# Two hybrid layers on one core: where key, query and output transposes and the conformer sums stand in PE's order

## What is computed

```python
for l in range(DEPTH):                         # DEPTH = 2
    u_lat = h_lat * (1.0 + scale) + shift      # the context likewise
    q, k, v, z_a, s_b, s_c, s_h, z_s, c_a, c_g, z_c, g_m = split(u_lat @ w_in[l])
    q, k = rope(rms_norm(q)), rope(rms_norm(k))          # 8 query heads, 2 key heads of 64
    o_attn = softmax(q @ k_all.T / 8) @ v_all            # keys: 256 context + 1024 latent
    br_a = (o_attn * silu(z_a)) @ w_pa
    br_b = (s_b * dwconv3(s_c * s_h) * silu(z_s)) @ w_ps
    hc = dwconv31(c_a * sigmoid(c_g)) + b_cdw
    hc = silu(layer_norm(hc, cln_g, cln_b))
    br_c = (hc * silu(z_c)) @ w_pc + b_pc
    merged = sigmoid(g_a) * br_a + sigmoid(g_b) * br_b + sigmoid(g_c) * br_c
    h_lat = layer_norm(alpha * h_lat + gate * (merged @ w_o), ...)
```

## Time and profile before

| | |
|---|---|
| median of 3 runs | 2879.9 us (2878.3 to 2881.78) |
| the profiled execution | 2872.59 us |
| its span, first to last instruction | 2870.8 us |
| mean granted PE clock | 0.978 |
| busy: PE, DVE, POOL, ACT | 93%, 53%, 32%, 29% |

### The profile page before, as it was taken

One profiled execution on the slowest core, in us unless ns is written; L12 is line 12 of the kernel. 1 busy time (PEld: TensorE's weight loads), 2 busy tenths in 40 slices (PEclk: granted clock), 3 DMA queues, 4 the chain that ended last, 5 costly groups with the idle time before them and its releaser, 6 DMA issues.

```text
span 2870.8 us, 32327 instructions
## 1 busy us (share of the span) xinstructions
PE 2677.8 (93%) x13560; PEld 2197.1 (77%) x13560; DVE 1511.9 (53%) x1410; ACT 820.9 (29%) x1156; POOL 907.0 (32%) x819
## 2 busy tenths in 40 slices
PE   7999999999999999999995899999999999999993
PEld 4778888887887888788883677777788888877882
DVE  3454444441019988845626444554540199875635
ACT  3234444442100000142213434444441000014313
POOL 3431111111225333334531342111113355544550
PEclk8999999999999999999998999999999999999996
DMA  6010110011241111133343311101012211123421
GB/s 253 30 61 34 34 37 34 34 43 57 75 163 65 32 43 38 48 118 121 128 162 133 135 48 46 40 34 41 34 41 81 74 52 44 45 70 125 144 95 66
DMA packets 65521, 212.12 MB, mean 74 GB/s; under 512 B 7520, under 2 KB 10848, under 8 KB 63328
## 3 DMA queue, kind: packets, MB, share of 16 engines
q1 hardware_dynamic: 47520, 179.11, 17.8%
q10 hardware_dynamic: 17856, 30.94, 2.9%
HBM read 164.93 MB, written 45.09 MB: 73 GB/s over the span
## 4 chain that ended last, share of the span: by engine, by line
PE 83%; DVE 7%; ACT 6%; issue 2%; DMA 1%; POOL 1%; SPq 0%; ACTq 0%; DVEq 0%; POOLq 0%
PE PS L695 46%; PE PS L824 19%; PE PS L855 5%; PE PS L864 5%; PE PS L877 5%; DVE cv L1487 2%; ACT Pr L1118 2%; ACT PTh L1138 1%; PE PS L887 1%; DVE qTl L1420 1%; DVE e L1555 1%; PE PS L736 1%; PE PS L742 1%; DMA wmA<-wmod 1%; DVE e L1563 1%
## 5 line engine op out<-in xcount | busy, mean ns | idle before, releaser
L584 POOL CAST wh<-wraw 128x512 fp32r<-128x512 f32 (+1 forms) x376 | 297.7, 792 | 1476.5 <-PE PS L695 805.6
L586 POOL TENSOR_TENSOR wl<-wraw,wh 128x512 fp32r<-128x512 f32 (+1 forms) x376 | 534.3, 1421 | 30.1
L1454 DVE TENSOR_TENSOR PTl<-PS,PTh 128x512 fp32r<-128x512 f32 x328 | 226.9, 692 | 423.1 <-ACT PTh L1138 423.1
L1487 DVE SCALAR_TENSOR_TENSOR cv<-hc,vec,cv 128x1024 f32<-128x1024 f32 x360 | 441.7, 1254 | 8.2
L695 PE MATMUL PS<-Uh,wh 128*128 128x512 f32 (+1 forms) x1536 | 428.3, 377 | 17.0 <-ACT Uh L1023 15.7
L695 PE MATMUL PS<-Uh,wl 128*128 128x512 f32 (+1 forms) x1536 | 420.1, 371 | 0.0
L695 PE MATMUL PS<-Ul,wh 128*128 128x512 f32 (+1 forms) x1536 | 418.9, 371 | 0.0
L824 PE MATMUL PS<-Uh,wh 128*128 128x512 f32 (+1 forms) x960 | 358.4, 373 | 1.2 <-ACT stg L1076 1.2
L824 PE MATMUL PS<-Ul,wh 128*128 128x512 f32 (+1 forms) x960 | 359.3, 374 | 0.0
L824 PE MATMUL PS<-Uh,wl 128*128 128x512 f32 (+1 forms) x960 | 359.0, 374 | 0.0
L1138 ACT ACTIVATE PTh<-PS 128x512 fp32r<-128x512 f32 x328 | 196.4, 599 | 480.0 <-PE PS L864 479.0
(11 more groups left out here) (153 smaller groups left out, 3275.8 us busy)
## 6 DMA issues: line engine op xcount, KB each, us to landing
wraw<-w SPq DMA_DIRECT2D x140, 512.0 KB, 3.4
graw<-stg ACTq DMA_DIRECT2D x96, 256.0 KB, 2.0
e<-graw SPq DMA_DIRECT2D x24, 640.0 KB, 3.9
wraw<-w SPq DMA_DIRECT2D x48, 256.0 KB, 4.1
wmL<-wmod SPq DMA_DIRECT2D x8, 1536.0 KB, 11.7
e<-graw SPq DMA_DIRECT2D x24, 512.0 KB, 3.6
wmA<-wmod SPq DMA_DIRECT2D x8, 1024.0 KB, 12.9
hL<-hT_in SPq DMA_DIRECT2D x8, 640.0 KB, 21.8
```

The costliest lines, as they stand in the source:

```text
L584: nc.gpsimd.tensor_copy(wh[par][:, s], wraw[par][:, s]).then_inc(whi[par], 1)
L586: nc.gpsimd.tensor_tensor(wl[par][:, s], wraw[par][:, s], wh[par][:, s].bitcast(F32), ALU.subtract).then_inc(wsplit[par], 1)
L1454: tt(PTl[b][:], PS[:, PT0[bank]:PT0[bank] + 512], PTh[b][:].bitcast(F32), ALU.subtract).then_inc(pt_free[bank], 1)
L1487: ins = stt(cv[:, i, c0:c0 + n], hc[:, i, CPAD * who + c0 + tap:CPAD * who + c0 + tap + n], vec[:, l, wt:wt + 1], cv[:, i, c0:c0 + n], ALU ...
```

## The change

Five things are changed.

1. **Keys and values from PSUM.** `k_hi` and the new `v_hi` copy each turned piece straight from PSUM to `kT` and `Vt`; `k_lo` and `v_lo` on DVE subtract piece by piece from PSUM, and it is DVE that frees the piece's bank. `raw` holds only k and the queries. `t_free` becomes two semaphores, one for each bank, with `wait_piece`.
2. **Key turns in job 3**, those of q1 in job 4 (job 0 is the first, so these are the fourth and fifth); ACT's and DVE's lists follow. On POOL the powers `rms(0)` and `rms(1)` move ahead of a split each (and of two table products in layer 0), and `split(j0 + 7)` behind `rms(4)`. `q_fill(0)` moves ahead of the third gate slice.
3. **In ten-step units** `back` and `q_fill` stand right behind `turn_probs`, and `q_hi` on ACT ahead of the exponential.
4. **Conformer sums.** The mean is computed inside the fourth z_c job, the variance inside merge job 2. ACT's root, DVE's reciprocal and all that follow are shifted to later merge jobs; so are the loads of `yA`.
5. **Merge jobs 8 and 16** wait for the operands of each k-step, not for all four.

```diff
-O_K, O_Q0, O_Q1, O_KT0, O_KT1, O_Q2, O_Q3, O_V = range(8)
+O_K, O_Q0, O_KT0, O_KT1, O_Q1, O_Q2, O_Q3, O_V = range(8)
...
+        def wait_piece(eng, f):
+
+            eng.wait_ge(t_free[f % 2], f // 2 + 1)
...
                     if q == 1:
                         load_gate(0)
                         load_gate(1)
+                    elif q > 1:
+                        load_gate(q)
+                    if q == 3:
                         load_ya(0)
                         load_ya(1)
-                    elif q > 1:
-                        load_gate(q)
-                    if q in (4, 5):
-                        load_ya(q - 2)
+                    if q in (5, 6):
+                        load_ya(q - 3)
...
+                rms(0)
                 split(j0 + 3)
...
-                rms(0)
+                rms(1)
                 split(j0 + 4)
                 split(j0 + 5)
-                rms(1)
                 rms(2)
                 split(j0 + 6)
-                split(j0 + 7)
                 rms(3)
                 rms(4)
+                split(j0 + 7)
...
-                job(j0 + 3, T, Uh, Ul, tokens_inside(O_Q1, (2, 3, 5)))
-                job(j0 + 4, T, Uh, Ul, keys_inside)
+                job(j0 + 3, T, Uh, Ul, keys_inside)
+                job(j0 + 4, T, Uh, Ul, tokens_inside(O_Q1, (2, 3, 5)))
...
                 for i in range(3):
                     to_tokens(O_V, i)
+                q_fill(0)
                 gate_slice(("a", 2))
                 wait_slot(pe, j0 + 5)
-                q_fill(0)
...
                     turn_probs(un, kt)
+                    if nk > 2:
+                        back_and_q(un, kt, nk)
                     if un + 1 < len(units):
                         for h in heads_at(nk, kt):
                             scores(un + 1, h)
                     if step >= 2:
                         pv(step - 2)
+                    gate_slice((un, kt))
                     if nk == 2:
-                        gate_slice((un, kt))
...
+                        back_and_q(un, kt, nk)
...
+                def mean_inside(k):
+                    if k in (2, 3, 5):
+                        pe.wait_ge(s_csum, 4 * l + 1)
+                        stat(l, O_CMEAN, e[4], ((2, 3, 5).index(k),))
+
+                job(j0 + I_ZC + 3, T, Uh, Ul, mean_inside)
+
+                def var_inside(k):
+                    if k >= 1:
+                        pe.wait_ge(s_csum, 4 * l + 2)
+                        stat(l, O_CVAR, e[5], (k - 1,))
...
+                    if q == 2:
+                        before = var_inside
                     if q == 8:
-                        pe.wait_ge(s_ya, KW * (l + 1))
+                        before = lambda k: pe.wait_ge(s_ya, KW * l + k + 1)
                     if q == 16:
-                        pe.wait_ge(s_yc, KW * (l + 1))
+                        before = lambda k: pe.wait_ge(s_yc, KW * l + k + 1)
...
+                def k_hi(g):
+                    for f, c, n in pieces(l, O_KT0 + g):
+                        act.wait_ge(t_done, f + 1)
+                        fn(kT[:, g, c:c + n], tbank(f, n), ACT.Copy).then_inc(s_khi, 1)
...
+                    if nk > 2 and un + 2 < len(units) and kt == q_at(nk):
+                        q_hi(un + 2)
                     if un + 1 < len(units):
                         for h in exps_at(nk, kt):
                             exps(un + 1, h)
-                    if un + 2 < len(units) and kt == q_at(nk):
+                    if nk == 2 and un + 2 < len(units) and kt == q_at(nk):
                         q_hi(un + 2)
...
                 silu_z(0)
                 silu_z(1)
+                silu_z(2)
                 mean(O_CMEAN, KW)
                 squares(12 * l, [cv[:, i, :T] for i in range(KW)])
-                silu_z(2)
                 silu_z(3)
-                root(O_CVAR, KW)
...
+                def k_lo(g):
+                    for i, (f, c, n) in enumerate(pieces(l, O_KT0 + g)):
+                        dve.wait_ge(s_khi, 6 * l + 3 * g + i + 1)
+                        tt(kT[HD:P, g, c:c + n], tbank(f, n)[HD:P], kT[HD:P, g, c:c + n].bitcast(F32),
+                           ALU.subtract).then_inc(t_free[f % 2], 1)
+                    wait_piece(dve, f)
                     dve.sem_inc(s_kv, 1)
...
                 mean_square(1, T)
+                k_lo(0)
+                k_lo(1)
...
-                    if q == 0:
+                    if q == 2:
+                        inverse_std(2 * l)
+                    if q == 3:
                         conf_norm(0)
                         conf_norm(1)
-                    if q == 1:
+                    if q == 4:
                         conf_norm(2)
                         conf_norm(3)
-                    if 2 <= q < 4:
-                        attn_lo(q - 2)
-                    if 2 <= q < 6:
-                        conf_out(q - 2)
+                        attn_lo(0)
+                        attn_lo(1)
+                    if q == 5:
+                        conf_out(0)
+                        conf_out(1)
+                    if q == 6:
+                        conf_out(2)
+                        conf_out(3)
```

More of the change, by code:

```diff
@@ L385, in build @@
         t_done = sem("piece_done")
-        t_free = sem("piece_read")
+        t_free = [sem(f"piece_read{i}") for i in range(2)]
         s_rawfree = sem("raw_free")
@@ L737, in turn_piece, with stat @@
                 ins.then_inc(t_done, 1)
-            def stat(l, op, src):
-                for f, c, n in pieces(l, op):
+            def stat(l, op, src, which=(0, 1, 2)):
+                for f, c, n in [p for i, p in enumerate(pieces(l, op)) if i in which]:
                     piece_wait(f)
@@ L889, in back, with back_and_q @@
                     ins.then_inc(pt_done[bank], 1)
+                def back_and_q(un, kt, nk):
+                    if un > 0 and kt == back_at(nk):
+                        back(un - 1)
+                    if un + 2 < len(units) and kt == q_at(nk):
+                        q_fill(un + 2)
                 wait_slot(pe, j0 + 4)
@@ L902, in _ @@
                     if h == 3:
-                        pe.wait_ge(t_free, last_piece(l, O_V) + 1)
+                        for f, _, _ in pieces(l, O_V):
+                            wait_piece(pe, f)
                         q_fill(1)
@@ L916, in _ @@
                         pv(step - 2)
+                    gate_slice((un, kt))
                     if nk == 2:
-                        gate_slice((un, kt))
-                    if un > 0 and kt == back_at(nk):
-                        back(un - 1)
-                    if un + 2 < len(units) and kt == q_at(nk):
-                        q_fill(un + 2)
-                    if nk > 2:
-                        gate_slice((un, kt))
+                        back_and_q(un, kt, nk)
                 pv(len(order) - 2)
@@ L947, in _ @@
                     if l == 0 and i == I_CONF + 4:
-                        pe.wait_ge(t_free, last_piece(l, O_OT + 3) + 1)
+                        for f, _, _ in pieces(l, O_OT + 3):
+                            wait_piece(pe, f)
                         for k in range(KD):
@@ L1084, in _ @@
                 evac(2)
-                square(O_Q1)
-                evac(3)
                 if l > 0:
                     act.wait_ge(s_hst, 16 * KD)
-                k_hi(O_KT0, 0)
-                k_hi(O_KT1, 1)
+                k_hi(0)
+                k_hi(1)
+                evac(3)
+                square(O_Q1)
                 evac(4)
@@ L1096, in _ @@
                 gate_out(("a", 1))
-                x = copy_raw(O_V)
-                fn(Vt[:, :, :, 0:HD], x[:].rearrange("p (t g d) -> p t g d", g=NKV, d=HD),
-                   ACT.Copy).then_inc(s_vhi, 1)
-                gate_out(("a", 2))
+                v_hi()
                 units = att_units(l)
@@ L1383, in q_out @@
                     return f
-                def k_lo(op, g):
-                    dve.wait_ge(s_khi, 2 * l + g + 1)
-                    st.done(tt(kT[HD:P, g, :], raw[op % 2][HD:P, :], kT[HD:P, g, :].bitcast(F32), ALU.subtract))
-                    dve.sem_inc(s_rawfree, 1)
+                def k_lo(g):
[4 more added lines that the diff above has]
+                    wait_piece(dve, f)
+                    dve.sem_inc(s_kv, 1)
@@ new lines, in v_lo @@
+                def v_lo():
+                    for i, (f, c, n) in enumerate(pieces(l, O_V)):
+                        dve.wait_ge(s_vhi, 3 * l + i + 1)
+                        tt(Vt[:, c // P:(c + n) // P, :, HD:P].rearrange("p t g d -> p (t g) d"),
+                           tbank(f, n).rearrange("p (h d) -> p h d", d=HD),
+                           Vt[:, c // P:(c + n) // P, :, 0:HD].rearrange("p t g d -> p (t g) d").bitcast(F32),
+                           ALU.subtract).then_inc(t_free[f % 2], 1)
+                    wait_piece(dve, f)
```

85 lines of the change are left out of this document (39 added, 46 removed).

## The result

The changed kernel takes 2833.4 us (median of 4 runs, 2829.1 to 2836.9) against 2879.1 us (2877.1 to 2881.8) for the kernel before beside it: a ratio of 0.984, 95% interval 0.982 to 0.986. Timed again on another occasion it was 2835.4 us, ratio 0.985 (0.984 to 0.987). The forecast was 2842, with a range of 2822 to 2864. The profiled execution has a span of 2834.3 us, 36.5 less than that of before.

What follows compares the result with a forecast made beforehand. PE, busy 93% of the span, bounds the kernel, so time comes only from its idle and low-clock stretches. Terms -21.1 - 30 + 3.7 - 7.7 + 17 = -38.1 take the median 2879.9 to 2842 us, range 2822 to 2864.

Steps and rivals of the forecast that it cites:

- Key transposes: Key turns in the fourth job, keys not using `raw`: stall chain gone, 10.4 + 9.2 = 19.6 us gained, bounds 0 to 19.6.
- The margin at the duplicated keys: Layer 1: duplicated keys must come 1.9 us sooner; POOL's earlier power leaves some 2.5 us margin, wider in layer 0.
- v and the first query: V's third piece waits longer, 1.5 us lost over both layers; the wait before the first scores is covered, 3.0 gained.
- The attention loop: Ten-step units: ACT's query copy ahead of the exponential gains 1.0 us in each of 30 units, -30 us, bounds 0 to -37.
- query at 1.13: Attention loop: ACT's query copy is done 1.13 us after the turn of probabilities starts, with scores at about 3.2.
- The zero: Attention loop, PE's output turns one step earlier: nothing waits for their operands, so 0; 1 us a unit if cover were gone.
- the 1.0: Attention loop: gain in us per unit, scores about 3.2 us after the turn of probabilities against 4.22 before.
- The short new wait for `Pr`: Attention loop: sign of being right, a short PE wait for `Pr` where the 37 us of `qTl` waits had stood.
- Conformer sums: Mean inside the fourth z_c job loses 1.8 and 2.6 us; with the variance together +3.7 us, bounds -4 to +7.
- The variance's part: Variance moved into the third merge job: -1.3 us in layer 0, +0.6 us in layer 1.
- `YAl` and the merge: Per-k waiting at the ninth merge job gains 7.7 us; late weights before the seventh cost 17 us, bounds 0 to 24.

Runs made afterwards that it cites:

- the run through `raw`: Changed kernel with the key turns back in the fifth job and keys through `raw` again, POOL's new order kept: 2838.5 us, ratio 0.987.
- The experiment: Changed kernel with SP issuing the weight loads of merge jobs 6 and 7 ahead of the third and fourth `yA` loads: 2818.1 us, ratio 0.980.
- ACT's copy undone: Changed kernel with only ACT's query copy put back behind the exponential, PE's new order kept: 2864.0 us, ratio 0.995.
- PE's order undone: Changed kernel with only PE's query refill and output turn put back behind the product with v, ACT's copy left early: 2844.7 us, ratio 0.988.
- the keys in the fifth job: Changed kernel with key turns back in the fifth job and q1's in the fourth, keys still straight from PSUM: 2833.4 us, ratio 0.984.
- the output copy: Changed kernel with ACT copying the last unit's output behind the exponential at step 1 of ten-step units: 2823.8 us, ratio 0.980.
- the mean: Changed kernel with the conformer mean put back as its own stretch between the second and third z_c jobs: 2832.1 us, ratio 0.984.
- the three together: Changed kernel with weights ahead of the `yA` loads, z_c evacuations freed by the last tap, and output copy behind the exponential: 2796.6 us, ratio 0.972.

## Why the prediction was right

**Key transposes.** The size held (-18.8 for -19.6). The reason is only half tested. The prediction listed the chain in full (piece, ACT, `raw`, the query normalisation, POOL's power) and then wrote "the keys use no `raw`, so the chain is gone". It counted POOL's reordering only as a margin for the duplicated keys. The change cuts the chain in two places, and the run through `raw` shows that the second cut is enough: with the power early, the normalisation reads `raw` in time and nobody waits for the buffer. So the prediction missed a cause that would have brought the gain by itself. Whether the one that it named would have done so too stays open, and that the size came out is no proof of its reason. The fourth job took 17.2 us from evacuation to evacuation, for 16.2, and the fifth 15.1, for 15.0.

**The margin at the duplicated keys.** The prediction called it wider in layer 0 than the 2.5 us of layer 1. It was the other way about: PE waits 0.81 us there and not at all in layer 1. The prediction had named such a wait as a sign of being wrong.

```profile
84.92 0.66 PE L741 MATMUL PS<-ident,kd 128*128 128x128 f32 x4 [0.81 <-DVE kd L1398]
```

DVE's two additions into `kd` took 1.49 us each in layer 1, 1.78 and 2.58 in layer 0 of before, and 4.13 and 4.25 now: they run beside POOL's two products for the rotation tables, which the move of the power had pushed there.

```profile
76.57 8.30 DVE L1398 TENSOR_TENSOR kd<-qa,qb 128x1280 f32<-128x1280 f32 x2
...
75.81 3.54 POOL L597 TENSOR_TENSOR e<-cosT,gain 128x1280 f32<-128x1280 f32 x1
79.31 4.21 POOL L597 TENSOR_TENSOR e<-sinT,gain 128x1280 f32<-128x1280 f32 x1
```

By the Trainium skill, SBUF — State Buffer, section SBUF: two separate sides, GpSimd and a VectorE operation with two SBUF inputs share one port pair, and whichever starts first keeps it for its whole instruction. The trace agrees: each addition grew by 2.6 to 2.8 us beside a product of 3.5 to 4.2, and ended 1.35 us after the product beside it, where an addition of this size takes 1.49 by itself.

**v and the first query.** The third pieces of v wait 1.42 and 1.63 us, for the 1.5 of the sum (0.75 today plus 0.75), and the first scores don't wait any more, in layer 0 or in layer 1 (1.50 and 1.46 us before).

**The attention loop.** -30 was forecast, 31 to 32 measured by stage (28 to 31 by medians), and the turn-to-scores time came out within 0.03 us. But the sum gave all of it to ACT and nothing to PE's new place. Its own step "query at 1.13" needs the query's turn finished by then, which at PE's old place it isn't (0.91 + 0.60 = 1.51). The zero was a condition of the 1.0, not a term beside it. The short new wait for `Pr` that was expected at this place didn't come; the 9.3 us there are those of before.

**Conformer sums.** The waits were forecast as 4.7 and 3.9 and are 4.09 and 3.79 us; the loss by the mean's move is 3.1 for 4.4. The variance's part wasn't measured by itself.

**`YAl` and the merge.** The waits for `YAl` are gone. The seventh merge job waits 6.47 and 5.81 us, for 6.3 and 7.0; with the 1.75 and 3.1 us lost to the clock behind them that is 17.1 us, for 17. (The experiment gained 17.3 with 3.2 us of waits left.) Inside it two sizes were off and cancelled: POOL had the weights 4.2 us after their issue, not 5.5, and then took 2.3 us for the first half of the split, not 1.2 (its cast 1.55). The Trainium skill, DMA: Bandwidth & Descriptors, section Queues, rings and completion order, says that completion isn't first-in first-out within an issuing engine. The traces don't show it: in those of before and of the changed kernel none of SP's 330 DMAs landed ahead of one issued before it. Here the weights landed 0.6 us behind the `yA` load that was issued just ahead of them and took 3.9; in the row that the prediction used that load took 5.2 and the weights 5.4.

**The level.** The sum missed the span difference by 1.6 us and the median difference (-45.7) by 7.6. A sum against one profiled execution is only as good as that execution is typical: the one of before was quick.

## What to carry to other kernels

Where a chain of waits ends in a stall and an edit touches two of its links, undo each by itself and then both before naming the cause; here the gain was credited to a freed buffer, and moving one small operation ahead of work that waits turned out to be enough, while what the freed buffer does alone was never tested. In a queue that runs in order, a load that must wait for a late consumer holds up every independent load behind it, so issue the independent ones first (17 us here for two loads). And when an edit is costed at nothing, look whether another term of the sum was worked out with that edit in place.

## What the hardware showed that was not expected

The same run of products has more than one pace at the full clock. In the layer-0 conformer stage PE does nothing but weight products, three chunks each, without a wait. In the first execution of before, then in the changed kernel (71 and 70 such products, first and last):

```profile
999.85 0.73 PE L695 MATMUL PS<-Ul,wh 128*128 128x512 f32 x3
...
1039.98 0.73 PE L695 MATMUL PS<-Uh,wh 128*128 128x512 f32 x3
```

```profile
999.73 0.74 PE L700 MATMUL PS<-Uh,wh 128*128 128x512 f32 x3
...
1039.98 0.75 PE L700 MATMUL PS<-Uh,wh 128*128 128x512 f32 x3
```

From start to start that is 40.13 / 70 = 0.573 and 40.25 / 69 = 0.583 us, with a granted clock of 1.00 in both; in the second execution of before it is (1040.36 - 999.76) / 70 = 0.580. Of the experiments those with ACT's copy undone, PE's order undone, the keys in the fifth job, the output copy and the mean had 0.573 here, the three together 0.580, and the others 0.583. So it doesn't go with the change, and it differs between two executions of the same kernel. With the waits taken off, the whole stage took 429.4 to 432.5 us in the six executions with 0.573 (the first of before and five experiments) and 434.0 to 435.9 in the eight others. That covers the 6.3 us that the changed kernel seemed to lose there, and a part of the 8.2 us between the two spans of before. What sets the pace stays open; no run here was made to find it.

The second is the cost of a wait beyond its length. In the changed kernel the 7 us behind PE waits of 3.8 to 6.5 us ran at 0.56 to 0.76 of the full clock; in the experiment with the weights first those behind waits of 1.1 and 2.2 us ran at 1.00. Between them either can happen: the wait ahead of the layer-1 mean was 2.74 us in the kernel before and 2.75 in the experiment with the mean as a stretch of its own, and the 7 us behind it were these:

```profile
2564.30:2571.30 7.00, 7.00 (x27) 5.08 (x28) 4.03 (x4) 5.02 (x6) 2.86 (x3) 1.00 0.33 87
```

```profile
2514.35:2521.35 7.00, 7.00 (x21) 4.49 (x22) 2.87 (x3) 4.65 (x6) 2.84 (x3) 0.79 0.33 89
```

Removing 7.9 us of waiting at the z_c jobs gave 12.7 us back, and removing 9.1 at the merge 17.3. The Trainium skill, TensorE: Matmul & The Clock Gate, section Part 1 (the HAM clock gate), says that the throttled clock is the default and that activity releases it. The trace agrees behind the four waits of 3.8 to 6.5 us; behind those of 1.1 and 2.2 us no fall is seen.
